# The output product of a filter network in rounded halves, with high and low rows stacked on the partitions

## The reference, cut to what matters

```python
h = jnp.sin(f_freq[0] * (z @ f_w_in + f_b_in))                      # 512 x 33 @ 33 x 64
for i in range(N_INNER_MLPS):                                       # two times
    h = jnp.sin(f_freq[i + 1] * (h @ f_w_mid[i] + f_b_mid[i]))      # 512 x 64 @ 64 x 64
h = (h @ f_w_out).astype(jnp.float32).reshape(L, 2, D_HYENA)        # 512 x 64 @ 64 x 1024
h = h * decay[:, None, :]
```

## Time and profile before

| | |
|---|---|
| median of 3 runs | 1547.76 us (1545.44 to 1547.87) |
| profiled execution, its time | 1549.24 us |
| profiled execution, its span | 1547.5 us |
| PE busy | 1502.6 us (97%) |
| PE weight loads busy | 1017.0 us (66%) |
| DVE busy | 664.0 us (43%) |
| POOL busy | 508.7 us (33%) |
| ACT busy | 506.0 us (33%) |
| HBM read | 303.39 MB |

### The profile page before, as it was taken

The page is one execution under the profiler, slowest core; times in us unless marked ns, Lnnn a source line. Parts: engine busy times, 40 slices in busy tenths (PEclk is TensorE's granted clock), DMA queues, the critical chain, the costliest instruction groups (busy, mean ns, idle before and its releaser), DMA issues.

```text
span 1547.5 us, 19352 instructions
## 1 busy us (share of the span) xinstructions
PE 1502.6 (97%) x7565; PEld 1017.0 (66%) x7566; DVE 664.0 (43%) x1136; ACT 506.0 (33%) x905; POOL 508.7 (33%) x326
## 2 busy tenths in 40 slices
PE   8999999999999999999999999999998998999997
PEld 6974667888788888888888777468543443443433
DVE  4155665132743333333345678664533232332334
ACT  4236665222543333321246433424111111111112
POOL 3443555444534444444714353622100010010000
PEclk9999999999999999999999999999999999999999
DMA  8333001222332222332223222368999999999995
GB/s 318 103 123 94 1 2 55 96 95 96 110 108 96 96 95 95 99 100 100 97 86 119 102 71 80 109 232 300 353 431 428 425 421 429 420 430 420 425 426 247
DMA packets 52059, 306.87 MB, mean 198 GB/s; under 512 B 7033, under 2 KB 7289, under 8 KB 38912
## 3 DMA queue, kind: packets, MB, share of 16 engines
q1 hardware_dynamic: 47296, 292.03, 48.8%
q0 software_dynamic: 4096, 11.49, 2.0%
q10 hardware_dynamic: 576, 2.10, 0.3%
HBM read 303.39 MB, written 4.19 MB: 199 GB/s over the span
## 4 chain that ended last, share of the span: by engine, by line
PE 82%; DMA 9%; DVE 5%; ACT 1%; issue 1%; POOL 1%; SPq 0%; DVEq 0%; ACTq 0%
PE banks L423 19%; PE banks L468 12%; PE banks L1243 12%; PE banks L426 9%; DMA ring<-experts 7%; PE banks L1276 5%; PE banks L1285 2%; PE banks L448 2%; PE banks L1044 2%; PE banks L2428 2%; DMA arena<-experts 2%; PE banks L2412 1%; PE banks L2399 1%; PE banks L2485 1%; PE banks L902 1%; PE banks L903 1%
## 5 line engine op out<-in xcount | busy, mean ns | idle before, releaser
L386 POOL TENSOR_TENSOR arena_r<-ring,arena_r 128x1024 fp32r<-128x1024 f32 x143 | 353.2, 2475 | 412.1 <-ACT arena_r L371 392.6
L371 ACT ACTIVATE arena_r<-ring 128x1024 fp32r<-128x1024 f32 x143 | 150.5, 1058 | 442.9 <-PE banks L426 279.5
L423 PE MATMUL banks<-hT_r,arena_r 128*128 128x512 f32 x640 | 250.0, 391 | 0.0
L423 PE MATMUL banks<-arena_r 128*128 128x512 f32 x640 | 249.1, 389 | 0.0
L1243 PE MATMUL banks<-ring,arena 128*64 128x512 f32 x704 | 225.6, 614 | 14.8 <-DMA ring<-experts 12.0
L468 PE MATMUL banks<-arena_r 128*128 128x512 f32 x784 | 183.5, 389 | 0.6 <-DVE arena_r L413 0.6
L1243 PEld LDWEIGHTS banks<-ring,arena 128*64 128x64 f32 x704 | 71.2, 141 | 147.3 <-issue 146.8
L468 PEld LDWEIGHTS banks<-arena_r 128*128 128x128 f32 x784 | 147.1, 188 | 31.5 <-POOL arena_r L386 1.0
L423 PEld LDWEIGHTS banks<-hT_r,arena_r 128*128 128x128 f32 x640 | 120.1, 188 | 29.1 <-issue 3.4
L423 PEld LDWEIGHTS banks<-arena_r 128*128 128x128 f32 x640 | 120.1, 188 | 25.1 <-issue 0.2
L426 PE MATMUL banks<-hT_r,arena_r 128*128 128x512 f32 x520 | 128.4, 389 | 0.0
(11 more groups left out here) (484 smaller groups left out, 2143.4 us busy)
## 6 DMA issues: line engine op xcount, KB each, us to landing
ring<-stream SPq DMA_DIRECT2D x164, 512.0 KB, 3.3
arena<-experts SPq DMA_DIRECT2D x35, 2048.0 KB, 15.8
ring<-experts SPq DMA_DIRECT2D x32, 2048.0 KB, 15.1
ring<-experts SPq DMA_DIRECT2D x18, 1024.0 KB, 17.9
arena<-experts SPq DMA_DIRECT2D x14, 1024.0 KB, 18.7
arena<-experts SPq DMA_DIRECT2D x25, 512.0 KB, 10.6
ring<-experts SPq DMA_DIRECT2D x12, 512.0 KB, 9.3
hT<-experts SPq DMA_DIRECT2D x8, 512.0 KB, 11.7
```

The costliest lines, as they stand in the source:

```text
L371: nc.scalar.activation(parts(name, m)[:, 0, :], tile(tile_n), ACT.Copy).then_inc(S["w_high"], 1)
L386: nc.gpsimd.tensor_tensor(w[:, 1, :], tile(tile_n), plain(w[:, 0, :]), ALU.subtract).then_inc(S["w_low"], 1)
L423: nc.tensor.matmul(pb[:, bank, :], w[:, 0, k * P:(k + 1) * P], b[:, k, :], start=(k == 0 and part == 0), stop=False)
```

## The change

The output product is done in fp32r parts. The third sine is computed twice, on partitions 0 to 63 and 64 to 127, since the weight of the last inner layer (`fw_last`) now has its 64 columns two times and bias and frequency are repeated. ACT rounds both copies to fp32r (`fh_split`); on the upper 64 partitions DVE then replaces the rounded value by the rest (`filter_lows`). So one operand holds the high rows below and the low rows above. The weight `fws` arrives on both halves of the partitions; ACT rounds it to `fws_high` (128 partitions), and POOL takes the rest of its lower half as `fws_lows` (64 partitions). For each output bank there is one product of 128 rows (`fh_split` by `fws_high`: high by high and low by high) and one of 64 rows (the high rows by `fws_lows`).

```diff
-        fws = ar(4096, 1024)
-        fzs = ar(5120, 512)
-        farg, fturn, fred, fh = [ar(512 * q, 512)[0:64, :] for q in range(4)]
+        fws, fw_last = ar(4096, 1024), ar(5120, P)
+        fzs = ar(5120 + P, 512)
+        farg, fturn, fred, fh = [ar(512 * q, 512) for q in range(4)]
+        fws_high, fws_lows, fh_split = fifth_r[:, 0:1024], fifth_r[0:64, 1024:2048], fifth_r[:, 3072:3584]
...
-            pool.dma_start(fws[0:64, :], fwout).then_inc(S["side_in"], 16)
+            pool.dma_start(ar(4096, 1024 + P), fwout).then_inc(S["side_in"], 16)
...
-            low_pool(pool, "in2", 2, 10)
-            pool.wait_ge(S["flt_act"], 3 + NT)
+            low_pool(pool, "in2", 2, 7)
+            pool.wait_ge(S["flt_act"], 3)
+            TT(fws_lows, fws[0:64, :], plain(fws_high[0:64, :]), ALU.subtract).then_inc(S["fws_low"], 1)
+            low_pool(pool, "in2", 7, 10)
+            pool.wait_ge(S["flt_act"], 5 + NT)
...
-                pe.wait_ge(S["flt_act"], 3)
-                if i >= 2:
-                    pe.wait_ge(S["flt_dve"], 3 + i - 1)
+                if i == 0:
+                    pe.wait_ge(S["fws_low"], 1)
+                pe.wait_ge(S["flt_dve"], 4 + max(i - 1, 0))
+                at = slice(i * P, (i + 1) * P)
                 for h in range(2):
-                    last = nc.tensor.matmul(pb[:, 4 + 2 * (i % 2) + h, :], fh[:, i * P:(i + 1) * P], fws[0:64, h * 512:(h + 1) * 512],
-                                            start=True, stop=True)
+                    half = slice(h * 512, (h + 1) * 512)
+                    nc.tensor.matmul(pb[:, 4 + 2 * (i % 2) + h, :], fh_split[:, at], fws_high[:, half], start=True, stop=False)
+                    last = nc.tensor.matmul(pb[:, 4 + 2 * (i % 2) + h, :], fh_split[0:64, at], fws_lows[:, half], start=False, stop=True)
...
-                    nc.scalar.activation(fh, fred, ACT.Sin).then_inc(S["flt_act"], 1)
+                    r = slice(0, 64 if n < 5 else P)
+                    nc.scalar.activation(fh[r, :], fred[r, :], ACT.Sin).then_inc(S["flt_act"], 1)
+                if n == 3:
+                    act.wait_ge(S["side_in"], 48)
+                    nc.scalar.activation(fws_high, fws, ACT.Copy).then_inc(S["flt_act"], 1)
+                if n == 5:
+                    act.wait_ge(S["flt_act"], 4)
+                    nc.scalar.activation(fh_split, fh, ACT.Copy).then_inc(S["flt_act"], 1)
...
+            def filter_lows():
+
+                dve.wait_ge(S["flt_act"], 5)
+                TT(fh_split[64:P, :], fh[64:P, :], plain(fh_split[64:P, :]), ALU.subtract).then_inc(S["flt_dve"], 1)
...
             filter_angle(2)
             convolve(5)
+            filter_lows()
             convolve(6)
```

More of the change, by code:

```diff
@@ L153 @@
 dve_chain proj_fm_ev proj_mla_ev proj_v_ev cmp_blocks cmp_gelu cmp_kv cmp_ready mla_stat mla_func mla_norm mla_tr mla_tr_ev mla_up mla_dve mla_act q_rope shift_in qk_in cs_pe cs_act cs_dve at_s at_max at_exp at_tr at_ev_dve at_ev_act at_pv at_o mg_sig mg_ev up_conv up_dve
-up_gelu up_g ple_mm ple_ev pg_mm pg_sig in2_lin in2_conv in2_f z_ready side_in flt_mm flt_act flt_dve
+up_gelu up_g ple_mm ple_ev pg_mm pg_sig in2_lin in2_conv in2_f z_ready side_in flt_mm flt_act flt_dve fws_low
 mixed tf_mm tf_act prod_ready y_ready combined yh_dve pool_chain hn_sq_f hn_sq_h hn_ms hn_rt hn_y
@@ L710, in second_pool @@
             pool.wait_ge(S["pool_chain"], 5)
-            pool.wait_ge(S["flt_dve"], 8)
+            pool.wait_ge(S["flt_dve"], 9)
             TT(x0t[:, :, :], x0t[:, :, :], by_channel(rsum_b), ALU.mult).then_inc(S["pool_chain"], 1)
@@ L915, in filter_layer @@
                     pe.wait_ge(S["flt_act"], q)
-                    w, u = col("f_w_mid", 64 * (q - 1), 64)[0:64, :], fh
+                    w, u = col("f_w_mid", 0, 64)[0:64, :] if q == 1 else fw_last[0:64, :], fh[0:64, :]
                 else:
@@ L919, in filter_layer @@
                     w, u = col("f_w_in", 0, 64)[0:33, :], fzs[0:33, :]
-                nc.tensor.matmul(pb[0:64, 5 + q, :], w, u, start=True, stop=True).then_inc(S["flt_mm"], 1)
+                nc.tensor.matmul(pb[0:64 if q < 2 else P, 5 + q, :], w, u, start=True, stop=True).then_inc(S["flt_mm"], 1)
             def filter_out(i):
-                pe.wait_ge(S["flt_act"], 3)
-                if i >= 2:
-                    pe.wait_ge(S["flt_dve"], 3 + i - 1)
+                if i == 0:
+                    pe.wait_ge(S["fws_low"], 1)
+                pe.wait_ge(S["flt_dve"], 4 + max(i - 1, 0))
+                at = slice(i * P, (i + 1) * P)
                 for h in range(2):
-                    last = nc.tensor.matmul(pb[:, 4 + 2 * (i % 2) + h, :], fh[:, i * P:(i + 1) * P], fws[0:64, h * 512:(h + 1) * 512],
-                                            start=True, stop=True)
+                    half = slice(h * 512, (h + 1) * 512)
+                    nc.tensor.matmul(pb[:, 4 + 2 * (i % 2) + h, :], fh_split[:, at], fws_high[:, half], start=True, stop=False)
+                    last = nc.tensor.matmul(pb[:, 4 + 2 * (i % 2) + h, :], fh_split[0:64, at], fws_lows[:, half], start=False, stop=True)
                 last.then_inc(S["flt_mm"], 1)
@@ L949, in second_pe @@
             pe.wait_ge(S["pool_chain"], 3)
-            pe.wait_ge(S["flt_dve"], 3 + NT)
+            pe.wait_ge(S["flt_dve"], 4 + NT)
             for h in range(2):
@@ L957, in second_pe @@
             pe.wait_ge(S["z_ready"], 4)
-            pe.wait_ge(S["flt_dve"], 8)
+            pe.wait_ge(S["flt_dve"], 9)
             tr_pe(pe, "z", uc[:, 4:8, :], 4, NT, bank0=4)
@@ L1367, in second_act @@
                     act.wait_ge(S["flt_dve"], n // 2 + 1)
-                    nc.scalar.activation(fh, fred, ACT.Sin).then_inc(S["flt_act"], 1)
+                    r = slice(0, 64 if n < 5 else P)
[6 more added lines that the diff above has]
+                    nc.scalar.activation(fh_split, fh, ACT.Copy).then_inc(S["flt_act"], 1)
                 if n == 7:
                     for i in range(NT):
-                        act.wait_ge(S["flt_dve"], 3 + i + 1)
+                        act.wait_ge(S["flt_dve"], 4 + i + 1)
                         if i >= 2:
@@ L1558, in filter_angle @@
                 b = col("f_b_in") if q == 0 else col("f_b_mid", q - 1)
-                L(TS(farg, pb[0:64, 5 + q, :], b[0:64, :], col("f_freq", q)[0:64, :], ALU.add, ALU.mult))
-                reduce_angle(L, nc, farg, fturn, fred)
-                TS(fred, fred, PI_LOW, -PI_LOW, ALU.min, ALU.max).then_inc(S["flt_dve"], 1)
+                r = slice(0, 64 if q < 2 else P)
+                L(TS(farg[r, :], pb[r, 5 + q, :], b[r, :], col("f_freq", q)[r, :], ALU.add, ALU.mult))
+                reduce_angle(L, nc, farg[r, :], fturn[r, :], fred[r, :])
+                TS(fred[r, :], fred[r, :], PI_LOW, -PI_LOW, ALU.min, ALU.max).then_inc(S["flt_dve"], 1)
+            def filter_lows():
+                dve.wait_ge(S["flt_act"], 5)
+                TT(fh_split[64:P, :], fh[64:P, :], plain(fh_split[64:P, :]), ALU.subtract).then_inc(S["flt_dve"], 1)
             def filter_rows(i):
@@ L1617, in second_dve @@
             filter_rows(3)
-            dve.wait_ge(S["flt_dve"], 3 + NT)
+            dve.wait_ge(S["flt_dve"], 4 + NT)
             TT(sums_pm[:, 0, :, :], HF[:, :, :], HB[:, :, :], ALU.add)
@@ L1622, in second_dve @@
             convolve(9)
-            dve.wait_ge(S["flt_act"], 3 + NT)
+            dve.wait_ge(S["flt_act"], 5 + NT)
             TT(turns_pm[:, :, 0:2, :], sums_pm[:, :, 0:2, :], sums_pm[:, :, 2:4, :], ALU.add)
@@ L3215 @@
          "pos_k": twice(a["nsa_pos_k"][0].T), "pos_v": twice(a["nsa_pos_v"][0].T),
-         "f_b_in": low(a["f_b_in_2"][0][:, None]), "f_freq": low(a["f_freq_2"][0].T), "f_b_mid": low(a["f_b_mid_2"][0].T),
+         "f_b_in": low(a["f_b_in_2"][0][:, None]), "f_freq": np.tile(a["f_freq_2"][0].T, (2, 1)), "f_b_mid": np.tile(a["f_b_mid_2"][0].T, (2, 1)),
          "f_w_in": low(a["f_w_in_2"][0]), "r_bias": np.broadcast_to(np.concatenate([a["b_group_2"][0], a["b_router_2"][0].reshape(-1)]), (P, 36)),
@@ L3226 @@
     ins["fconst"], ins["decay"] = filter_tables()
-    ins["fwout"] = a["f_w_out_2"][0]
+    ins["fwout"] = np.tile(np.concatenate([a["f_w_out_2"][0], *[a["f_w_mid_2"][0, 1]] * 2], axis=1), (2, 1))
     ins["frow"] = np.broadcast_to(a["f_bias_2"][0], (P, CH))
```

## The result

The changed kernel is slower. Its median is 1551.52 us (1548.8 to 1552.95, 11 runs) against 1546.32 us for the kernel before in the same rounds (11 runs, one of them of 5315.39 us, the others 1542.81 to 1548.68); the ratio is 1.0037, with a 95% interval of 1.0029 to 1.0045, so 5.7 us (4.5 to 7.0 us). I had forecast 1549.4 us, in a range up to 1551.8 us, as 1.7 us more than before: no change that can be told. Two later sets of runs with the same kernel gave 1.0035 (1.0023 to 1.0047) and 1.0046 (1.0032 to 1.0060).

What follows compares the result with a forecast made beforehand. It took PE's chain to bound the kernel from 855 to 960 us, with all changes reaching the end: +2.2 us of waiting and -0.54 us of products, +1.7 us on 1547.76 us, so 1549.4 us, range 1545.0 to 1551.8 us.

Steps and rivals of the forecast that it cites:

- What bounds the kernel: PE is the chain without a gap between 855 and 960 us; all of a change there reaches the end.
- The products: PE's output pairs: fp32r work plus 8 row-count changes of 0.225 us, 3.62 against 3.89 us per pair, 0.54 us less in all.
- Rivals 1 and 4: Row-count changes free: with DVE delayed, -1.9 us, chance 0.13; with neither cost there, -4.1 us, chance 0.06.
- The filter weight, the copy on ACT, the doubled sine: Larger weight transfer, ACT's 1.06 us copy in a hole, third sine on 128 partitions: all costed at nothing.
- POOL's subtraction and DVE: POOL's step behind tile 6 delays DVE's angle by 4.2 us, so PE waits 2.2 us ahead of its first output product.
- Rival 2: DVE isn't delayed beyond PE's step 6 and row changes cost as forecast: -0.5 us, 1547.2 us, chance 0.10.
- rival 3: `filter_lows` falls under POOL's tile 8, PE idles 5.4 us and the clock falls: +7.9 us, 1555.6 us, chance 0.10.
- The clock: PE's clock falling to 1.2 GHz behind an idle gap: up to 3 us more, counted in rival 3 only.
- The sum against the time of the runs: +1.7 us added to the median of the runs, 1547.76 us, gives 1549.4 us; profiled span forecast 1549.2 us.
- Rival 5: PE changes as forecast, but the expert stage gives or takes the difference, so the end stays: 1547.8 us, chance 0.09.

Runs made afterwards that it cites:

- full rows: Changed kernel with the second product of each bank also on 128 rows: 1.0012 to the kernel before; with the low part of the weight also early, 0.9998.
- low part early: Changed kernel with ACT's rounding of the filter weight and POOL's subtraction moved ahead of the `in2` tiles: 0.9998 to the kernel before.

## Why the prediction was wrong, step by step

**What bounds the kernel.** Right: PE is the chain from 855 to 958 us, and what is lost there reaches the end.

**The products.** Right in mechanism, and too small by 0.36 us. I had 0.225 us for a change of rows and -0.54 us for both pairs; the runs show 0.20 us and -0.90 us. Rivals 1 and 4, with free changes, are refuted by the products that start 0.43 us apart, and 0.23 us apart with full rows.

**The filter weight, the copy on ACT, the doubled sine.** Right: none of them shows in the chain. With the low part early, the same fetch and the same copy cost nothing.

**POOL's subtraction and DVE.** Right, almost to the row: line 3062 stopped, line 3066 moved under tile 7, `filter_lows` done just ahead of tile 8, and the wait 2.2 us as summed (1.97 us of idling, and a first product of 0.47 us where 0.23 us are usual). Rival 2 (DVE isn't delayed) and rival 3 (`filter_lows` under tile 8) did not happen.

**The clock: the step that failed.** The sum took the wait at its length. I had the clock in rival 3 alone and let it come in only at a gap of 5.4 us, because the kernel before shows full speed behind 1.60 us and a low clock behind 3.33 us. A gap of 2.2 us lies between these two rows, so by my own rule it had to be bounded from both sides: 0 and 3.0 us. I priced it at nothing and gave the bound to another case. It cost 3.06 us, more than the wait of 2.19 us. With that term the sum is 2.2 - 0.54 + 3.06 = +4.7 us, the forecast 1552.5 us and slower the likeliest sign. The rows at 1179.81 and 1310.91 also stand among other work than the filter's, and the runs show how little the length of a gap alone says: full speed behind 0.84 us and a low clock behind 0.1 us, and both behind 2.03 us. Why the clock falls behind one gap and not behind another stays open; that it fell here, and what it cost, is shown.

**The sum against the time of the runs.** I added to the median of three runs, and the profile of before had those 3.5 us in the expert stage, so the agreement of the two spans (1549.1 us, 1549.2 us forecast) is an accident. So is it that the measured 1551.52 us lies just below the end of my range, 1551.8 us: the median that I added to, 1547.76 us, was 1.4 us above the one of the same rounds. The 5.7 us are also 1.3 us more than the stretch lost; where those are is open, as said above, and they lie within the interval.

**Rival 5** (the end doesn't move) is refuted by the medians, +5.4 to +7.1 us in three sets of runs and -0.3 us once the stretch is short again.

## What to carry to other kernels

Before a step is put into a hole of POOL's list, look at what DVE does in that hole: one POOL step of 2.4 us delayed DVE's chain by 4.2 us, and moving it 30 us ahead gave all of it back. A short wait on PE is not worth its length only: where a profile shows a low clock behind some gap, put its price in the sum for every gap that isn't shown to be harmless at that place. And products that alternate between 64 and 128 rows pay 0.2 us for each change, nearly as much as an fp32r product of 512 columns, so filling the upper rows with something harmless or useful can be the better form. It pays only if the other engines keep up with the faster PE: here POOL's list didn't, and the gain came with its new order.

## What I had not expected of the hardware

Gap and clock don't go together in a simple way. With two added steps on DVE 8 products ran slowly in both profiles, with three none in three profiles, though the gap is the longer one; and the gap of 2.03 us ahead of tile 13 had a low clock behind it in one kernel and full speed in the other.

The clock falls late, not at the gap: 1.65 us after the work had begun again in the first profile of the changed kernel, about 1.3 and 2.4 us in its two later ones, 3.4 to 3.7 us with two added steps. So which products are slow differs between executions of one kernel, while what they lose together hardly does: the stretch is 101.74, 101.69 and 101.77 us.
